# One weight chunk of the first expert group in scratch space, and the gate weights half a slot on, in a streamed mixture-of-experts trunk

## What is computed

```python
for layer in range(DEPTH):                      # 2 layers
    hn = rms_norm(h, attn_norm_g[layer])
    mix = mixer_ab(...) if layer % 2 == 0 else mixer_c(...)
    h = h + mix
    h = h + hierarchical_moe(rms_norm(h, ffn_norm_g[layer]), ...)
return rms_norm(h, final_norm_g)

def expert_block(args):                         # for every expert e
    xb, e = args
    h = jax.nn.silu(xb @ w_gate[e]) * (xb @ w_up[e])
    return h @ w_down[e]
```

## Time and profile before

| | |
|---|---|
| median of 3 runs | 1119.46 us |
| the profiled execution: span, first to last instruction | 1120.8 us |
| TensorE matmul busy | 827.4 us (74%) |
| read from HBM | 436.60 MB, 390 GB/s over the span |
| ScalarE, VectorE, GpSimd busy | 157.8, 195.7, 58.7 us |
| layer 0: mixer, then experts | 0 to about 157 us, then to about 585 us |
| layer 1: mixer, then experts | to about 682 us, then to about 1110 us |

### The profile page before, as it was taken

How to read it: one execution, slowest core, us unless ns; L and a number is a source line. 1 busy time by engine, 2 the same in 40 slices (tenths; PEclk the granted TensorE clock), 3 DMA queues, 4 the chain that set the end, 5 groups by cost and what they waited for, 6 DMA issues and landing times.

```text
span 1120.8 us, 13766 instructions
## 1 busy us (share of the span) xinstructions
PE 827.4 (74%) x5882; PEld 460.5 (41%) x5882; DVE 195.7 (17%) x498; ACT 157.8 (14%) x365; POOL 58.7 (5%) x81
## 2 busy tenths in 40 slices
PE   9999999746575566648789999956556565746876
PEld 8888774312222131314447776331313122311533
DVE  2546441000000000000018635100000000000002
ACT  2225233000000000000011545100000000000102
POOL 1010020000000000000000442000000000000000
PEclk9999999968787797869989999977888777877989
DMA  9952779999999999999999659999999999999994
GB/s 377 429 210 95 308 308 424 426 443 440 417 427 443 431 431 429 441 433 428 423 418 421 249 205 372 422 436 438 436 420 430 440 436 417 427 439 440 428 425 185
DMA packets 22640, 438.37 MB, mean 391 GB/s; under 512 B 2624, under 2 KB 3648, under 8 KB 6336
## 3 DMA queue, kind: packets, MB, share of 16 engines
q1 hardware_dynamic: 21328, 434.39, 91.5%
q10 hardware_dynamic: 1264, 3.27, 0.7%
HBM read 436.60 MB, written 1.05 MB: 390 GB/s over the span
## 4 chain that ended last, share of the span: by engine, by line
DMA 53%; PE 43%; DVE 1%; issue 1%; ACT 1%; SPq 0%; POOL 0%; DVEq 0%; ACTq 0%; POOLq 0%
DMA store<-in_w_down 21%; DMA store<-in_w_gate 18%; PE bank L1438 18%; DMA store<-in_w_up 13%; PE bank L1110 5%; PE bank L1101 5%; PE bank L1270 5%; PE bank L1581 1%; PE bank L1041 1%; PE bank L1070 1%; PE bank L1374 1%; PE bank L1362 1%; PE bank L1461 1%; PE bank L1204 0%; PE bank L1182 0%
## 5 line engine op out<-in xcount | busy, mean ns | idle before, releaser
L1438 PE MATMUL bank<-store,hg 128*32 128x512 f32 x2048 | 279.9, 704 | 208.9 <-DMA store<-in_w_up 109.8
L1438 PEld LDWEIGHTS bank<-store,hg 128*32 128x32 f32 x2048 | 72.3, 127 | 399.1 <-issue 258.7
L1438 PE MATMUL bank<-store 128*32 128x512 f32 x880 | 120.8, 702 | 63.9 <-DMA store<-in_w_down 62.5
L1438 PEld LDWEIGHTS bank<-store 128*32 128x32 f32 x880 | 34.2, 126 | 142.8 <-issue 141.1
L2028 DVE TENSOR_TENSOR store<-store,bank 128x512 f32<-128x512 f32 x14 | 9.6, 687 | 465.7 <-PE bank L1438 465.7
L1270 PE MATMUL bank<-store 128*128 128x256 f32 x256 | 64.8, 389 | 0.5 <-ACT store L995 0.5
L1101 PE MATMUL bank<-hg,store 128*128 128x256 f32 x256 | 57.1, 383 | 0.3 <-DMA store<-w_ab 0.3
L1362 PEld LDWEIGHTS bank<-store,hr 128*128 128x128 f32 x448 | 51.5, 193 | 13.1 <-issue 13.1
L1362 PE MATMUL bank<-store,hr 128*128 128x128 f32 x448 | 54.2, 280 | 0.0
L2035 DVE COPY hg<-bank 128x512 f32<-128x512 f32 x14 | 9.7, 692 | 248.6 <-PE bank L1438 248.6
L1461 PE MATMUL bank<-store,hg 128*128 128x256 f32 x224 | 50.8, 380 | 1.4 <-ACT store L902 1.4
(11 more groups left out here) (248 smaller groups left out, 688.2 us busy)
## 6 DMA issues: line engine op xcount, KB each, us to landing
store<-in_w_up SPq DMA_DIRECT2D x12, 4096.0 KB, 24.7
store<-in_w_down SPq DMA_DIRECT2D x20, 2048.0 KB, 24.2
store<-in_w_gate SPq DMA_DIRECT2D x14, 2048.0 KB, 12.5
store<-in_w_up SPq DMA_DIRECT2D x13, 2048.0 KB, 17.1
store<-in_w_down SPq DMA_DIRECT2D x6, 4096.0 KB, 23.8
store<-in_w_down SPq DMA_DIRECT2D x14, 1024.0 KB, 27.7
store<-w_ab SPq DMA_DIRECT2D x6, 2048.0 KB, 30.6
store<-in_w_up SPq DMA_DIRECT2D x5, 1024.0 KB, 5.5
```

Of the source, the lines that this page charges most:

```text
L1438: op = pe.matmul(dst[rows, :], lhsT[:, q, rows], moving, start=(q == 0), stop=(q == steps - 1))
```

## The change

The first quad's gates are laid half a slot on: chunk 0 sits in the upper half of slot 3, chunks 1 and 2 fill slot 4, chunks 3 and 4 slot 5, chunks 5 and 6 slot 6. The lower half of slot 3 is free for the upper half of unit 11, which is loaded in the mixer, together with the gates. The last gate chunk (7) is loaded in two pieces of 0.5 MB into places that nothing else uses at that time: piece 0 at the start of the desk (where `e_h` and `e_hT` now lie, which moved ahead of `pick`), during the mixer; piece 1 in the lower half of `hg`, as soon as its tokens are transposed. The second quad's gates lie in the same manner, with chunk 7 in the lower half of slot 10, and their loads are released by other counters.

```diff
+        last_gate = [arena[:, UNIT:UNIT + 2 * DE], flat(hg[:])[:, 0:2 * DE]]
...
+        def gate_chunk(l, q, n=1):
+            lo = LOOP_SLOTS[l][0] * UNIT + (q + 1) * HALF_UNIT
+            return store[:, lo:lo + n * HALF_UNIT]
...
+            def first_gate(l, j):
+                landed = moe[l]["landed"][j]
+                if j == 0:
+                    sp.dma_start(gate_chunk(l, 0), gate_chunks(l, 0, 0)).then_inc(landed, 16)
+                    sp.dma_start(home(LOOP_SLOTS[l][0])[:, 0:HALF_UNIT],
+                                 units(l, 0, QUAD_UNITS - 1)[:, HALF_UNIT:UNIT]).then_inc(landed, 16)
+                else:
+                    sp.dma_start(gate_chunk(l, 2 * j - 1, 2), gate_chunks(l, 0, 2 * j - 1, 2)).then_inc(landed, 16)
+
+            def last_first_gate(l, part):
+                src = gate_chunks(l, 0, KD - 1)[:, part * 2 * DE:(part + 1) * 2 * DE]
+                sp.dma_start(last_gate[part], src).then_inc(last_gate_landed, 16)
@@ experts(l) on SP
                 sp.dma_start(flat(hT[:]), last_rows[:, 0:HALF_UNIT]).then_inc(m["low_landed"], 16)
+                sp.wait_ge(hr_turned, 4 * l + 2)
+                last_first_gate(l, 1)
                 sp.wait_ge(m["low_used"], 1)
-                sp.dma_start(home(LOOP_SLOTS[l][0])[:, 0:HALF_UNIT], last_rows[:, HALF_UNIT:UNIT]).then_inc(m["landed"][0], 16)
+                sp.dma_start(gate_chunk(l, 0), gate_chunks(l, 1, 0)).then_inc(early_up[1], 16)
                 sp.wait_ge(m["low_used"], 2)
...
+                sp.dma_start(gate_chunk(l, 1), gate_chunks(l, 1, 1)).then_inc(m["landed"][ring_place((0, 0), 0)[0]], 16)
+                for j, done, count in ((1, m["used"], 1), (2, m["low_used"], 3), (3, m["used"], 3)):
+                    sp.wait_ge(done, count)
+                    sp.dma_start(gate_chunk(l, 2 * j, 2), gate_chunks(l, 1, 2 * j, 2)).then_inc(
+                        m["landed"][ring_place((0, 0), j)[0]], 16)
+                for j in range(QUAD, QUAD_UNITS):
+                    if j in (5, 7, 9):
+                        sp.wait_ge(m["used"], {5: 4, 7: 6, 9: 7}[j])
                     load(l, 1, j, ring_place((0, 0), j)[0])
@@ layer 0, behind the mixer's last weights
-            for j, u in ((7, 2), (0, 3), (1, 4), (2, 5), (3, 6)):
-                sp.wait_ge(ab["used"], u + 1)
-                first(0, j)
+            sp.wait_ge(ab["used"], 3)
+            first(0, 7)
+            for j in range(QUAD):
+                sp.wait_ge(ab["used"], j + 4)
+                first_gate(0, j)
...
             first(0, 5)
+            last_first_gate(0, 0)
@@ layer 1
-                        first(1, j)
+                        first_gate(1, j)
...
             part_of_up(1, 6, HALF_UNIT, HALF_UNIT + D)
+            last_first_gate(1, 0)
             sp.wait_ge(cc["out"], KD)
@@ first_gates() on TensorE
+                            elif q < KD - 1:
+                                pe.wait_ge(m["landed"][(q + 1) // 2], 16)
+                            else:
+                                pe.wait_ge(last_gate_landed, 32 * (l + 1))
...
-                    gates(2, 3, "xe_high", 1).then_inc(m["low_used"], 1)
-                    gates(3, 4, "xe", 3).then_inc(m["used"], 1)
+                    pe.wait_ge(m["xe_high"], 1)
+                    gates(2, 3)
+                    pe.wait_ge(m["xe"], 3)
+                    gates(3, 4).then_inc(m["used"], 1)
```

More of the change, by code:

```diff
@@ L358, in hybrid_trunk @@
             "chosen", "ranked", "fullest", "fullest_row", "rounds")}
+        last_gate_landed = sem("last_gate_landed")
         early_up = [sem(f"early_up{j}") for j in range(2)]
@@ L531, in first, with gate_chunks @@
                 load(l, 0, j, ring_place(0, j)[0])
+            def gate_chunks(l, quad, q, n=1):
+                return weights[0][l, quad][:, q * HALF_UNIT:(q + n) * HALF_UNIT]
+            def first_gate(l, j):
[9 more added lines that the diff above has]
+                sp.dma_start(last_gate[part], src).then_inc(last_gate_landed, 16)
             def part_of_up(l, j, lo, hi, last=False):
@@ L1378, in first_gates, with gates @@
                 def first_gates():
-                    def gates(lo, hi, copied, count):
-                        pe.wait_ge(m[copied], count)
-                        return four(0, 0, bank[6], xeT, KD, slice(0, DE), part=(lo, hi))
+                    def gates(lo, hi):
+                        for q in range(lo, hi):
+                            if q == 0:
+                                pe.wait_ge(m["landed"][0], 32)
+                            elif q < KD - 1:
+                                pe.wait_ge(m["landed"][(q + 1) // 2], 16)
+                            else:
+                                pe.wait_ge(last_gate_landed, 32 * (l + 1))
+                            for s in range(QUAD):
+                                rows = slice(s * CAP, (s + 1) * CAP)
+                                at, place = (gate_chunk(l, q), s) if q < KD - 1 else (last_gate[s // 2], s % 2)
+                                op = pe.matmul(bank[6][rows, :], xeT[:, q, rows], at[:, place * DE:(place + 1) * DE],
+                                               start=(q == 0), stop=(q == KD - 1))
+                        return op
@@ L1384, in first_gates @@
                     gather_first(0)
                     gather_first(1)
[L1386 removed]
+                    pe.wait_ge(m["xe"], 1)
+                    gates(0, 1).then_inc(m["low_used"], 1)
                     gather_first(2)
                     gather_first(3)
[L1389 to L1391 removed]
+                    pe.wait_ge(m["xe"], 2)
@@ L1392, in first_gates @@
+                    gates(1, 2).then_inc(m["low_used"], 1)
+                    pe.wait_ge(m["xe_high"], 1)
+                    gates(2, 3)
+                    pe.wait_ge(m["xe"], 3)
+                    gates(3, 4).then_inc(m["used"], 1)
                     gather_first(4)
                     gather_first(5)
-                    gates(4, 6, "xe_high", 2).then_inc(m["low_used"], 1)
-                    gates(6, 8, "xe_high", 3).then_inc(m["used"], 1)
+                    pe.wait_ge(m["xe_high"], 2)
@@ L1397, in four @@
+                    gates(4, 6).then_inc(m["low_used"], 1)
+                    pe.wait_ge(m["xe_high"], 3)
+                    gates(6, 8).then_inc(m["used"], 1)
                 def four(place, kind, dst, lhsT, steps, cols, part=None):
@@ L1430, in four @@
                                 half = home(slot(c))[:, q % 2 * HALF_UNIT:(q % 2 + 1) * HALF_UNIT]
-                                if place != 0 and singly(place) and c == 0:
-                                    half = (home(LOOP_SLOTS[l][0])[:, HALF_UNIT:UNIT], home(slot(0))[:, 0:HALF_UNIT])[q]
+                                if kind == 0 and place != 0 and singly(place):
+                                    half = gate_chunk(l, q)
                                 moving = half[:, s * DE:(s + 1) * DE]
```

13 lines of the change are left out of this document (1 added, 12 removed).

## The result

The changed kernel takes 1114.45 us, the median of 4 runs (1112.19 to 1115.24), and the kernel before 1119.03 (1117.78 to 1119.86, 4 runs). The ratio is 0.9947, with a 95% interval of 0.9932 to 0.9962: 5.9 us less, 4.3 to 7.6 (the medians alone are 4.6 apart). Two later sets gave 0.9954 [0.994, 0.9968] and 0.9953 [0.9941, 0.9964], with medians 5.0 and 5.3 us apart. The forecast was 3.5 less, 1116.0 us, with a range from 1114.2 to 1119.0.

What follows compares the result with a forecast made beforehand. The prediction took the DMA stream, never dry in the experts' phases, to bound the kernel. Gains of 2.45 (layer 0) and 1.3 (layer 1) less 0.25 made 3.5 us, from 1119.46 to 1116.0 us, range 1114.2 to 1119.0.

Steps and rivals of the forecast that it cites:

- What bounds the kernel: Experts' phases of both layers: the DMA queue never runs dry, share 1.00 at 430 GB/s from 230 to 580 us.
- Layer 0, 2.45: Layer 0's stream starts at 164 us as before with 1 MB less behind it: 2.45 us gained.
- Layer 1, 1.3: Layer 1 from 673 us on: same bytes loaded, only the hole at 688 to 690 goes, 1.3 us gained.
- Two small transfers, 0.25 lost: Layer 1's stream: two 0.5 MB transfers in place of one of 1 MB cost 0.25 us.
- What was added in places said to be covered: Later gate releases, TensorE's new wait at chunk 7 and SP's two more DMAs per layer: zero cost.
- Both layers fully, 4.9: Rival: layer 1's stream had hidden room between 673 and 688 us; gain 4.9 us, time 1114.6, chance 0.08.
- The dry queue: Rival: layer 0's shorter queue runs dry, at most 2.45 us given back; time 1118.2, chance 0.18 (with a lower rate).
- the late piece: Rival: piece 1 lands late and TensorE stalls at chunk 7 in both layers; 11.9 us slower, 1131.4, chance 0.06.
- the small transfers on their own: Rival: layer 1's two small transfers cost 2.35 us each; 1.0 us slower, time 1120.4, chance 0.04.

Runs made afterwards that it cites:

- l0_only: The change in layer 0 alone, layer 1 as in the kernel before: 1118.05 us, ratio 0.9985.
- A: Not a run: time in a profile from layer 0's `hT` load to the start of TensorE's last row of downs in layer 0.
- C: Not a run: time in a profile from layer 1's `hT` load to the start of the last row of downs; 424.4 us with old layers, 420.6 with new.
- l1_only: The change in layer 1 alone, layer 0 as in the kernel before: 1116.75 us, ratio 0.9967.
- before_again: The kernel before, unchanged, run and profiled once more: 1120.0 us in one run, span 1118.0.
- after_again: The changed kernel, unedited, run and profiled once more: 1114.78 us, against 1119.75 for the kernel before measured beside it.
- late_l1: The changed kernel, but layer 1's load behind the former hole waits until half of the first quad's gates are used: 1116.42 us, ratio 0.9962.
- no_pieces_l1: The changed kernel without layer 1's two 0.5 MB loads of the last gate chunk, and without TensorE's wait for them: 1115.44 us, ratio 0.9952.
- B: Not a run: time in a profile from the start of TensorE's last row of downs in layer 0 to layer 1's `hT` load.
- before_warm: The kernel before with 8 small dummy matmuls on TensorE ahead of the last wait for a down in each layer: 1122.38 us, ratio 1.0015.
- after_third: The changed kernel, unedited, measured and profiled a third time: 1115.12 us, ratio 0.9953.
- late_l0: The changed kernel, but in layer 0 the second quad's gate chunk 0 is issued 2 us later, together with chunk 1: 1114.69 us, ratio 0.9953.

## Why the prediction came out as it did

**What bounds the kernel: right.** From 230 to 580 us the changed kernel streams as before. Here is this stretch, with the place of layer 0's last hole and layer 1's start:

```profile
150.06:165.06 15.00, 14.46 (x105) 11.66 (x107) 7.05 (x33) 5.24 (x14) 3.60 (x5) 1.00 0.78 292
162.00:164.00 2.00, 2.00 (x17) 1.12 (x16) 0.58 (x3) 0.24 (x1) 0.00 (x0) 1.00 0.92 373
165.06:178.06 13.00, 13.00 (x121) 5.22 (x117) 4.28 (x36) 7.33 (x13) 0.62 (x1) 1.00 0.96 374
230.00:580.00 350.00, 219.61 (x1714) 95.64 (x1710) 13.87 (x22) 17.08 (x34) 3.70 (x6) 0.82 1.00 429
672.26:687.26 15.00, 14.38 (x112) 11.51 (x115) 10.50 (x42) 8.92 (x23) 5.83 (x8) 1.00 1.00 413
687.26:700.26 13.00, 13.00 (x121) 5.24 (x117) 4.29 (x36) 5.92 (x12) 0.62 (x1) 1.00 1.03 431
672.26:717.26 45.00, 43.69 (x371) 24.27 (x374) 17.35 (x80) 16.80 (x39) 7.07 (x10) 1.00 1.01 423
```

and the same stretches of the kernel before, counted from its own `hT` loads:

```profile
149.94:164.94 15.00, 14.45 (x105) 11.67 (x107) 7.03 (x33) 5.25 (x14) 3.60 (x5) 1.00 0.65 225
164.94:177.94 13.00, 13.00 (x121) 5.24 (x117) 4.28 (x36) 7.32 (x13) 0.61 (x1) 1.00 1.01 412
675.02:690.02 15.00, 14.38 (x112) 11.51 (x115) 10.49 (x42) 8.92 (x23) 5.83 (x8) 1.00 0.94 368
690.02:703.02 13.00, 13.00 (x121) 5.25 (x117) 4.29 (x36) 5.92 (x12) 0.61 (x1) 1.00 0.99 384
675.02:720.02 45.00, 43.68 (x371) 24.29 (x374) 17.33 (x80) 16.80 (x39) 7.06 (x10) 1.00 0.98 396
```

**Layer 0, 2.45: right in kind, too large.** The hole at 162 to 164 was filled (107 to 373 GB/s), and the 15 us up to it took in (292 - 225) x 15 = 1.0 million bytes more, the whole moved megabyte. But "the stream starts at 164 as before, with 1 MB less behind it" took for granted that it would then run at 412 again. The next 13 us ran at 374 (366 to 401 in the six profiles with the new code, 398 to 419 in four with the old): 0.49 million bytes less in this pair, 1.1 us. What is left is 1.2 by this pair; on the means of the six and the four profiles (371 and 355 GB/s over 45 us) it is 1.7. l0_only gave 1.7, and A fell by 2.0 on the mean of five profiles with exactly this code in layer 0 (420.71 to 422.92). The forecast 2.45 still lies inside l0_only's interval (0.6 to 2.8), so it is the rates, not the time, that show it as too large.

**Layer 1, 1.3: the step that failed.** "From 673 us to the end the kernel loads the same bytes as before; only the hole goes. Gain 1.3." The bytes are the same, but the hole cost more than its own 1.35 us: the 12 us behind it at 378 GB/s were its after-effect (377 to 408 in the four profiles with the old layer 1, so this one was the slowest). They lack (428 - 378) x 12 = 0.6 million bytes, 1.4 us. Hole and after-effect make 2.75. The 45 us stretch says the same: (423 - 396) x 45 = 1.2 million bytes, 2.8 us; on the mean of four old and eight new profiles (399 and 422) 2.5. C puts the layer's whole gain higher, at 3.8, and l1_only at 3.7 (3.0 by the medians). The microsecond between is not in the long stretch: the 374 us from 38 us behind the `hT` load on run at 431 GB/s with either code. It is at the end of the stream. The 3 us and the 5 us that begin 417 and 420 us behind the load, in before_again and then in after_again:

```profile
1097.04:1100.04 3.00, 2.82 (x49) 1.53 (x44) 0.00 (x0) 0.93 (x3) 0.00 (x0) 1.00 0.83 341
1100.04:1105.04 5.00, 4.05 (x68) 2.03 (x64) 0.00 (x0) 0.59 (x2) 0.00 (x0) 1.00 0.21 84
```

```profile
1096.01:1099.01 3.00, 2.61 (x44) 1.19 (x36) 0.00 (x0) 0.38 (x1) 0.00 (x0) 1.00 0.40 164
1099.01:1104.01 5.00, 3.94 (x79) 2.53 (x82) 1.33 (x4) 1.75 (x7) 0.00 (x0) 1.00 0.02 3
```

In before_again 1.44 million bytes are left, which would take 3.3 us at 430 GB/s, and the last row of downs starts 6.65 us on. In after_again it is 0.51 million, 1.2 us, and the row starts 3.56 us on. So 3.3 us are lost there with the old code (3.8 and 4.6 in l0_only and before) and 2.4 with the new (four profiles): the DMA engines end less together, at a share of 0.21 instead of 0.02 in the last 5 us. late_l1, whose edit brings a hole back, is at 0.23 there; but no_pieces_l1 has one too and is at 0.03. Why the end is uneven stays open.

**Two small transfers, 0.25 lost: wrong in sign, and the same mistake.** I read the 378 GB/s as the price of small transfers and charged it per transfer. The changed kernel has two of those three 1 MB transfers and the same 2 MB ones in the same 13 us, behind two of half a megabyte, and runs at 431. The price per transfer was also worked out wrongly: 12 us at 378 GB/s move 4.5 million bytes, which is three transfers of 1 MB and most of one of 2 MB, and not six. The Trainium skill, "DMA: Bandwidth & Descriptors", section "Bandwidth", asks for at least 1 MiB per transfer. In a queue that others keep filled this case shows no cost of 0.5 MB transfers: the 15 us that begin 9 us ahead of the `hT` load hold both of them and run at 407 GB/s, against 401 in the kernel before. The reading that would have told the two apart was in the rows: 673 to 688 held small transfers too, and ran at 400, and layer 0's stream behind its own hole, with three 1 MB transfers as well, ran at 415.

**What was added in places said to be covered: right.** TensorE's last half of the first quad's gates, where chunk 7 stands, and the row behind it:

```profile
168.79 3.20 PE L1423 MATMUL bank<-store,hg 128*32 128x512 f32 x26
171.40 0.60 PE L1423 MATMUL bank<-hg 128*32 128x512 f32 x2
```

Neither has a wait. Layer 0's refill came in time too: 177 to 180 us moves 421 GB/s, where the prediction named under 400 as the sign of a dry queue.

**A term that wasn't in the sum: TensorE's clock at the end of layer 0.** The last two rows of matmuls on TensorE's time line ahead of layer 1's mixer, in the kernel before:

```profile
580.91 1.94 PE L1479 MATMUL bank<-store 128*32 128x256 f32 x16 [2.16 <-DMA store<-in_w_down]
582.78 2.66 PE L1499 MATMUL bank<-hg 32*128 32x256 f32 x32
```

and its stretch of those rows, with the granted clock third from the end:

```profile
580.90:585.40 4.50, 4.49 (x48) 2.61 (x48) 0.00 (x0) 0.38 (x1) 0.00 (x0) 0.64 1.06 436
```

The same rows in before_again, which is the same kernel:

```profile
580.46 1.07 PE L1479 MATMUL bank<-store 128*32 128x256 f32 x16 [1.00 <-DMA store<-in_w_down]
581.46 2.01 PE L1499 MATMUL bank<-hg 32*128 32x256 f32 x32
```

and its stretch:

```profile
580.40:583.50 3.10, 3.01 (x48) 1.96 (x48) 0.00 (x0) 0.38 (x1) 0.00 (x0) 1.00 1.05 424
```

After a wait of 2.16 us the clock is for most of both rows at its lower level (1.2 of 2.4 GHz; 0.64 is the mean over them), and from the start of the first to the end of the second they take 4.53 us. After a wait of 1.00 it stays at 1.00, and they take 3.01. The 1.5 us between are the difference in B. l1_only, also with the old layer 0, waited 2.46 us and lost the same; none of the ten profiles with the new layer 0 did, whose waits there were at most 1.00 us. With the old layer 0 it was two of four; the other two are before_again, and before_warm, where the fillers stood in the wait. If half of the old executions pay it, it is 0.75 us of the gain, an estimate. That the change brings the shorter wait is a count of profiles, not something that a run isolated.

**The sum again.** From the runs 1.7 + 3.7 = 5.4 us by the ratios, with the clock's part inside the first, against 5.2 to 5.9 measured; by the medians 1.7 + 3.0 = 4.7, against 4.6 to 5.3. For the pair of first profiles, by the table: A and B 525.08 to 522.20, 2.9; C 4.75; the `hT` load of layer 0 0.1 later; together 7.5.

**The rivals.** "Both layers fully, 4.9" came nearest the time, largely by luck. Its reason, room in layer 1's stream between 673 and 688, holds for 6 GB/s (401 to 407), 0.2 us; the larger room lay behind the hole and at the stream's end, and layer 0 gave less than its full 2.45. The dry queue, the late piece and the small transfers on their own didn't occur.

## What to carry to other kernels

A hole in a DMA stream can cost more than its own length, when the stream behind it is slower while loads come in one by one: about 1.1 us more in layer 1 of the old code here (393 GB/s for 13 us, against 431), 0.6 in layer 0 (410). So look at the GB/s of the 10 to 15 us behind a hole against the long stretches before pricing a change that closes it, and don't trust the DMA share: it read 1.00 at 391 GB/s and 1.03 at 431. Where a rate has two possible causes (size of transfers, depth of the queue), look for a second stretch in which only one of them holds. And compare executions from landmarks that no edit moves, since profiled spans of one kernel differed here by 2.8 us.

## What the runs showed of the hardware

- Rate behind a hole, by what is queued at the restart: 4 MB released within a microsecond, 431 GB/s 2 us later (late_l1); loads of 1 MB released one by one, 384 to 399 for 13 us in layer 1 and 398 to 419 in layer 0 (old code, four profiles each). Without a hole and with 0.5, 1 and 2 MB transfers mixed: 413 over 15 us and then 431 over 13 (layer 1, changed kernel).
- Where the stream ends, the DMA engines don't end together: the last 5 us ran at a share of 0.19 to 0.25 in the four profiles with layer 1's old code, and of 0.01 or 0.02 in six with the changed kernel's layer 1. The difference comes to 0.9 to 2.2 us.
- Around a 1 MB load that joins an almost drained queue the stream can be slow: 246 and 279 GB/s over 4 us at shares of 1.08 and 0.74 (after_third), where the same load issued 2 us later, after a hole, ran at 287 and then 438 (late_l0). The cause is open, and the time was the same.
- TensorE's last wait for a down was 0.97 to 1.00 us in layer 0 of ten profiles and 0.93 to 0.95 in layer 1 of two profiles each of both kernels, whatever the stream did. Fillers in its place made the kernel 1.8 us slower, so this isn't time that other work can use without checking what it delays.
